# Modulation blocks spread over five feed-forward parts and both of their products

## The reference, cut to what matters

```
for each of the 10 sublayers s:      # mla ffn fourier ffn | ffn mix ffn  ffn mix ffn
    shift, scale, gate = split(silu(c) @ ada_w[s] + ada_b[s], 3)    # 1024 x 3072 weights
    h = norm(x) * (1 + scale) + shift
    if ffn:   y = (silu(h @ w1) * (h @ w3)) @ w2                    # 1024 -> 2816 -> 1024
    else:     y = attention and convolution / Fourier mixer / token mixer
    x = x + gate * y            # the second model scales x and norms the sum
```

## Time and profile before

| | |
|---|---|
| median of three runs | 2341.11 us (2326.58 to 2344.95) |
| the profiled execution | 2341.43 us, its span 2339.5 us |
| busy over the span | PE 2218.7 us (95%), DVE 773.7 (33%), ACT 356.4 (15%), POOL 119.3 (5%) |
| mean granted clock of PE | 0.976 |
| transfers | 438.27 MB, mean 187 GB/s |
| chain that ended last | PE 74% of the span, DMA 18%, DVE 5% |

### The profile page before, as it was taken

How to read it: one execution, slowest core, us unless ns; L and a number is a source line. 1 busy time by engine, 2 the same in 40 slices (tenths; PEclk the granted TensorE clock), 3 DMA queues, 4 the chain that set the end, 5 groups by cost and what they waited for, 6 DMA issues and landing times.

```text
span 2339.5 us, 23963 instructions
## 1 busy us (share of the span) xinstructions
PE 2218.7 (95%) x10232; PEld 1876.4 (80%) x10232; DVE 773.7 (33%) x1601; ACT 356.4 (15%) x667; POOL 119.3 (5%) x231
## 2 busy tenths in 40 slices
PE   7899997999997999899999999799999999999997
PEld 4677886868876888688688888688888868888886
DVE  5545344012442034315533434312001453341002
ACT  3334100022000000013221200001000323120001
POOL 0000011000110011100000011100000000000000
PEclk9899998999998999899999999899999999999998
DMA  9563588423785478643333378653434333334431
GB/s 376 190 243 108 190 328 302 151 108 144 298 301 196 180 264 315 241 155 144 139 131 143 126 264 319 216 181 135 154 124 156 140 131 144 123 130 159 154 124 68
DMA packets 61539, 438.27 MB, mean 187 GB/s; under 512 B 6976, under 2 KB 8768, under 8 KB 39552
## 3 DMA queue, kind: packets, MB, share of 16 engines
q1 hardware_dynamic: 28608, 318.35, 36.7%
q0 software_dynamic: 32256, 117.45, 14.1%
q10 hardware_dynamic: 576, 1.05, 0.1%
HBM read 434.72 MB, written 2.10 MB: 187 GB/s over the span
## 4 chain that ended last, share of the span: by engine, by line
PE 74%; DMA 18%; DVE 5%; issue 1%; ACT 1%; SPq 0%; ACTq 0%; POOL 0%; DVEq 0%
PE lin L1444 58%; DMA ada_ring<-in_ada 17%; PE small_ps L1444 4%; DVE ada_ring L864 4%; PE lin L1759 2%; PE lin L1702 1%; DMA rec<-in_ada_pe 1%; PE small_ps L1778 1%; PE lin L1716 1%; PE lin L1656 1%; PE small_ps L1548 1%; PE small_ps L1669 1%; PE lin L1724 1%; PE small_ps L1750 0%; PE lin L1584 0%
## 5 line engine op out<-in xcount | busy, mean ns | idle before, releaser
L1444 PE MATMUL lin<-h,ring 128*128 128x256 f32 x5424 | 1183.8, 380 | 20.8 <-ACT rec L811 8.4
L1444 PEld LDWEIGHTS lin<-h,ring 128*128 128x128 f32 x5424 | 1031.5, 191 | 168.2 <-issue 10.0
L1444 PE MATMUL lin<-big,ring 128*128 128x256 f32 x2112 | 466.2, 384 | 49.8 <-DVE big L1405 49.8
L1444 PEld LDWEIGHTS lin<-big,ring 128*128 128x128 f32 x2112 | 407.1, 193 | 108.9 <-DVE big L1405 52.2
L864 DVE CUSTOM_DVE_ANT_0 ada_ring<-ada_ring,crow 128x1024 f32<-128x1024 f32 x224 | 271.9, 1224 | 278.0 <-DMA ada_ring<-in_ada 276.6
L997 DVE SCALAR_TENSOR_TENSOR x<-lin,mod,x 128x256 f32<-128x256 f32 x80 | 38.7, 484 | 526.0 <-PE lin L1444 500.9
L463 POOL DMA_DIRECT2D ada_ring<-in_ada x224 | 118.8, 531 | 1374.2 <-DVE sums L864 1336.1
L828 ACT ACTIVATE sil<-lin 128x256 f32<-128x256 f32 x112 | 43.0, 384 | 734.0 <-PE lin L1444 700.8
L1405 DVE TENSOR_TENSOR big<-sil,lin 128x256 f32<-128x256 f32 x112 | 46.9, 419 | 317.7 <-ACT sil L828 317.7
L1444 PE MATMUL lin<-rec,ring 128*128 128x257 f32 (+1 forms) x608 | 142.9, 386 | 7.8 <-ACT rec L526 7.8
L1444 PEld LDWEIGHTS lin<-rec,ring 128*128 128x128 f32 x608 | 117.1, 193 | 26.9 <-issue 9.6
(11 more groups left out here) (296 smaller groups left out, 1165.9 us busy)
## 6 DMA issues: line engine op xcount, KB each, us to landing
ring<-in_w SPq DMA_DIRECT2D x66, 2048.0 KB, 8.2
ada_ring<-in_ada POOLq DMA_DIRECT2D x224, 512.0 KB, 6.9
ring<-in_w SPq DMA_DIRECT2D x48, 1408.0 KB, 6.1
ring<-in_gates SPq DMA_DIRECT2D x12, 2048.0 KB, 8.0
ring<-in_mproj SPq DMA_DIRECT2D x8, 2048.0 KB, 8.1
ring<-in_mtok SPq DMA_DIRECT2D x4, 2048.0 KB, 7.7
ring<-in_branch SPq DMA_DIRECT2D x4, 2048.0 KB, 7.7
ring<-in_wout SPq DMA_DIRECT2D x4, 2048.0 KB, 7.7
```

The source lines that it names most:

```text
L1444: ins = mm(dst, w[:, lo:lo + m], rhs(k), start=k == 0, stop=k == nk - 1)
```

## The change

The 224 blocks stay the same, and so does their order. Where DVE takes them changes: of the 15 before the keys, 2 instead of 5 stand before the context is normed; the 192 of the feed-forward parts go to the first five such parts (sublayers 1, 3, 4, 6, 7) as 48, 48, 32, 32, 32, of each five eighths in w13 (units 2 to 21) and three eighths in w2 (after units 0 to 5). PE sums the squares of the context between the two halves of the first unit. ACT issues the four stores of the bias rows at the beginning of `mla`, after the context, instead of each right after its copy.

```diff
-ADA_BEFORE_CONTEXT, ADA_BEFORE_KEYS, ADA_AFTER_KEYS = 5, 15, 9
-ADA_IN_MLA, ADA_IN_FFN = ADA_N - FIRST_GATE + ADA_N, 2 * ADA_N
+ADA_BEFORE_CONTEXT, ADA_BEFORE_KEYS, ADA_AFTER_KEYS = 2, 15, 9
+ADA_IN_MLA = ADA_N - FIRST_GATE + ADA_N
+ADA_PER_FFN = [48, 48, 32, 32, 32, 0]
...
                     A(rows, pa[a][:], ACT.Copy).then_inc(s_bias_row_taken, 1)
-                    act.wait_ge(s_bias_row_taken, nth(act, s_bias_row_taken))
+
+            def bias_rows_stored():
+
+                act.wait_ge(s_bias_row_taken, nth(act, s_bias_row_taken, AH))
+                for a in range(AH):
+                    rows = tok[:].rearrange("p a b -> p (a b)")[:, a * 512:(a + 1) * 512]
                     act.dma_start(bias_rows[a, 0:P * 512].rearrange("(p s) -> p s", s=512), rows)\
                        .then_inc(s_bias_rows_dma, 16)
...
+                bias_rows_stored()
                 latent(u, [(proj[:, 12], 0, T, col("q_norm", 0)), (proj[:, 13], T, 2 * T, col("q_norm", 1))], sq[:, 0:2])
...
+            def share(blocks_in_all, parts, n):
+
+                return blocks_in_all * (n + 1) // parts - blocks_in_all * n // parts if n < parts else 0
+
+            def ffn_before(s):
+
+                return subs[:s].count("ffn")
...
                         dve.wait_ge(s_tiles_added, nth(dve, s_tiles_added))
+                    if name == "w2":
+                        ada(share(ADA_PER_FFN[ffn_before(s)] * 3 // 8, KD - 2, m))
                 dve.wait_ge(*taken(u0 + KD - 1))
...
-                        if n >= RAW:
-                            ada(ADA_IN_FFN * (n + 1 - RAW) // (KF - RAW) - ADA_IN_FFN * (n - RAW) // (KF - RAW))
+                        ada(share(ADA_PER_FFN[ffn] * 5 // 8, KF - 2, n - 2) if n > 1 else 0)
...
                 tile_sum(b[:, 0:T], w, 0, KD, lat)
+                squares_summed()
                 tile_sum(b[:, T:2 * T], w, KD * P, KD, lat).then_inc(s_unit, 1)
-                squares_summed()
```

## The result

The changed kernel takes 2272.8 us (median of 4 runs, 2271.99 to 2274.54); the kernel before, run beside it, 2342.76 (4 runs, 2326.58 to 2344.95). The ratio is 0.9717, with a 95% interval of 0.9673 to 0.9761: faster by 2.8%. The profiled execution of the changed kernel took 2274.54, its span is 2272.5; that is 66.9 us less than the profiled execution before, where the sum said 73.9. One run of the kernel before, beside `e5` to `e8`, took 2390.18 us, some 45 above the others, and is left out of the ratios there.

What follows compares the result with a forecast made beforehand. It took late block loads in crowded w13 stretches, plus PE's wait for the context, to bound the kernel. Feed-forward 61.6, context 9.9 and stores 2.4 sum to 73.9 us off 2341.4: 2268 us, range 2258 to 2286.

Steps and rivals of the forecast that it cites:

- What bounds the kernel: In w13 of sublayers 1, 3, 4 and 6, too many block loads beside the ring's; PE stood 56.9 us for DVE.
- w13, 52.9 us: Lateness from the fifth unit to w2 in sublayers 1, 3, 4 and 6, against sublayer 7: 52.9 us together.
- w2, 8.7 us: w2 behind the four waits is slower than sublayer 7's 76.25 us; this goes with the gap, 8.7 us in all.
- The count of the demand: w2 with three blocks per unit asks 316 GB/s; blocks keep up, at 2.7 us each, 8.1 of the unit's 9.53.
- Part 2: At the context in the beginning: 8.4 us of waiting and 1.5 of slower instructions go, 9.9 us, with 0.6 to spare.
- The cover at the keys: DVE, 10.5 us late at the keys if blocks land no sooner, is covered by 14.41 us of standing, 4 left.
- Part 3: Four 256 KB stores in the first 28 us, moved later, let loads behind them come sooner: 2.4 us, bounds 0 and 2.5.
- The sum: Over the whole kernel, 61.6 + 9.9 + 2.4 = 73.9 us off 2341.4, giving 2267.5, said as 2268.
- Rival (b): Blocks late in w2 of sublayers 1 and 3: 2289 us, or 2278 if DVE holds POOL up; chance 0.11.
- Rival (c): Blocks late at the end of w2 in five parts, slower than before: 2383 us at 15 us a round; chance 0.02.
- Rival (a): The beginning gives little, 0 to 5 us instead of 9.9 at the context: 2273 to 2278 us; chance 0.14.
- Rival (d): Something hidden, such as the ring, holds PE; w13 keeps some 10 us in four parts: 2308 us; chance 0.03.

Runs made afterwards that it cites:

- e5: The changed kernel with the same 48, 48, 32, 32, 32 blocks per feed-forward part, but all in w13 and none in w2: 2282.25 us.
- e8: The changed kernel with five blocks ahead of the context again instead of two: 2281.11 us.
- e1: The kernel before with only the new distribution of blocks in the feed-forward parts: 2283.23 us.
- e6: The changed kernel with blocks moved from w13 to w2: four per w2 unit in sublayers 1, 3 and 7, six in 4, three in 6: 2310.14 us.
- e7: The changed kernel with the squares of the context summed behind the second half of the first unit again: 2278.43 us.
- e9: The changed kernel with the four stores of the bias rows issued early again, as before: 2275.24 us.
- e4: The changed kernel with unread products in sublayers 4 to 9, four ahead of the wait for the sum of the squares, six behind the mean: 2265.83 us.
- e11: The changed kernel with only the six unread products behind the mean, in sublayers 4 to 9: 2265.47 us.
- e12: The changed kernel with only the four unread products ahead of the mean, in sublayers 4 to 9: 2268.5 us.
- e2: The kernel before with only the changed beginning (two blocks before the context, squares between the halves, stores late), feed-forward parts as before: 2335.02 us.
- e10: e4 with ten more unread products ahead of the first products on h: 2265.64 us.

## Why the prediction was right, point by point

It said 2268, 2258 to 2286, and faster by over 1%; measured were 2272.8 and 2274.38. By its steps:

- **What bounds the kernel:** right. With the blocks spread, the waits of PE for `big` and DVE's waits for blocks went together (56.9 to 7.9 us, 276.6 to 26.1), and `e1` alone does it.
- **w13, 52.9 us:** 52.7 measured. **w2, 8.7 us:** 8.8 measured. That w2's slowness goes with the gap ahead of it is shown by `e5`, where w2 is slow (77.64, 78.99) only behind the two late w13.
- **The count of the demand:** right in what it decided. Asked for 316 GB/s, w2 got 305 with no wait on DVE; `e6` shows the edge at four per unit (327 GB/s) and a price of 2.6 us per block at six. The pace of 2.7 us per block was misread: the earlier trace rows has 44 blocks in the 129.48 us, 2.9 each, and `e5` has one in 3.0. Three are then 8.8 us and not 8.1, still under the 9.53 of a unit, so the conclusion stood, with less room than the working says.
- **Part 2, 9.9 us, margin 0.6:** the 8.4 us of waiting are gone and the cause is as stated; `e7` and `e8` give its two halves (3.2 and 7.2). The margin was about the 0.6 forecast: the last context tile is done at 55.68 (its row of ACT starts at 55.19 and takes 0.49) and PE comes to it near 56.2. It was not the second block that set it, as the deviation came 4.0 us after DVE was free. The term that was mis-sized is the 1.5 us for slower instructions. Behind the context they are gone, but the first 16 instructions on `h` now take 5.38 us, 1.8 too long. The change didn't make that: `e1`, with the old beginning, has it too (8.83 us for 32), and so has every trace in which that stop of 2.75 us isn't filled, but for the one before. The 7.15 of the earlier trace rows, from which the working went, were the lucky case.
- **The cover at the keys:** right, and narrow. DVE comes to the keys at 88.39, behind its last block, with its input there since 78.96: 9.4 us late, where 10.5 was named as the case with loads no sooner. PE isn't held, and the 14.41 us in which DVE stands for PE afterwards are still there.

```profile
88.39 0.29 DVE L1046 TENSOR_REDUCE sd<-proj 128x4 f32<-128x128 f32 x1
```

- **Part 3, 2.4 us:** 2.05 at the first products on `h`, and 1 to 2.5 by `e9`. By the 358 GB/s of the Trainium skill (SBUF — State Buffer, Summary: rules for kernel authors) the estimate would have been 2.9, and the runs can't tell 2.4 from 2.9; that rate isn't this core's limit, though, which moved 425 GB/s.
- **The sum:** the missing 7 us are, in this trace, 5.3 behind the norms and 1.9 at the beginning, both of one kind (the second is within the scatter of the mark). The working took for granted that stretches which the change doesn't touch keep their clock. They didn't: stops of 1.10 and 1.55 us (1.46 and 1.55 ahead of sublayer 6 before) were followed by a slow stretch in two or three of five sublayers before, and in five of five after. This is the step that was off, and `e4`, `e11` and `e12` show what it cost behind the norms by taking the slowness away and nothing else.
- **Rival (b), late at three blocks per w2 unit:** fell. DVE's idle time there is 0.0. An issue of POOL takes 528 ns in the mean over all 224, and 528 in the w2 with three blocks per unit, 531 before. The lock that the Trainium skill describes (SBUF — State Buffer, SBUF: two separate sides) holds for DVE operations in a fast mode with two ports; if this one were such, the issues beside it would have grown, and they didn't. **Rival (c):** its mechanism is real, at six blocks per unit (`e6`), with the size that its formula gives (a round of 15.4 us ends 6 x (15.4 - 9.53) - 9.5 = 25.7 us late, and PE stood 23.7). **Rival (a):** the context came early enough. **Rival (d):** no ring load was hidden behind the wait.

What stays open: why the clock falls behind those norms in nearly every case once the blocks are redistributed (the changed kernel twice, `e1` and `e5` to `e9`: 39 of 40 take 5.19 us or more, one 3.72), but in only two or three of five in the kernel before and in `e2` (3.72, 5.12, 3.72, 5.21, 5.24), with the stop for the scaled tile as long in all. The traces of the ten kernels without fills narrow it down. Behind the mixers (sublayers 6 and 9) it is slow everywhere, 20 of 20, old distribution or new. The difference is behind a w2 (sublayers 5, 7 and 8): 23 of 24 with the new distribution, 1 of 6 with the old. The work of PE ahead doesn't tell the cases apart: in sublayer 7 it is alike in the two kernels (125.62 and 125.59 us of w13, 76.25 of w2), and yet sublayer 8 starts with 3.71 us before and 5.40 after. The blocks beside that work aren't needed for it either: `e2` has none there and takes 5.21. Also open is why the kernel before scatters over 30 us from run to run (2326.58 to 2358.13), and `e2` over 17, while the others stay within 5; both have the late w13, which points there without showing it.

## What to carry to other kernels

When one engine waits for loads in a few crowded stretches and has room in others, count the demand per unit of time of each stretch (bytes of all queues by the stretch's length) and compare it with what the fullest stretch was seen to move; here up to 305 GB/s was free, 327 was at the edge. Add to each gap that goes the slow instructions behind it, and don't book a gain in clock at a place where a short stop remains. Short stops of the matmul engine can cost again behind them, here 1.68 us behind stops of 1.10 and 1.55, and a handful of products that nobody reads, placed in them, won 8.5 us of 2274.

## What the hardware showed that I had not expected

- The same stops, 1.10 and 1.55 us with 0.70 us of work between, are followed by the full clock in one kernel (16 instructions in 3.72 us) and by a granted clock of 0.50 in another (5.40 us). Filling either of the two is enough nearly always: 3.72 us in five of five with the second filled, in four of five with the first.
- The narrow products (128x32) run partly slow though PE doesn't stop in them: 32 instructions take 3.65 us and then the next 32 take 5.13 in the changed kernel, 6.61 in `e10`. The granted clock falls while PE is busy all the time, to 0.66 in the mean from 74 to 79 us:

```profile
73.51 5.13 PE L1587 MATMUL lin<-ring,rec 128*128 128x32 f32 x32
...
74.00:79.00 5.00, 5.00 (x31) 4.93 (x31) 3.40 (x7) 0.32 (x2) 1.58 (x3) 0.66 0.58 179
```

- 32 blocks in w2 and w13 of sublayer 7, which had none, cost 0.0 us on PE: 125.59 us against 125.62, and 76.25 both times. (What changed is the first unit behind it, 5.40 us instead of 3.71.)
